# Six open blocks in the first stage of a decoder trunk, with two waits re-ordered around them

## The reference, cut to what matters

```
mod = silu(c) @ ada_w[l] + ada_b[l]            # six vectors: shift, scale, gate, twice
h = rms_norm(x, norm_mix_g[l]) * (1 + scale) + shift
u = h @ w_in                                    # 1024 x 3072: Bg, Cg, xv
z = Cg * xv;  y = (Bg * conv3(z)) @ w_out;  x = x + gate * y
...
q, k, v = projections per head pair; p = softmax(q k^T / 8 + F[t] - F[s]); o = p v
```

## Time and profile before

| | |
|---|---|
| median of 3 runs | 1160.84 us (1160.73 to 1161.4) |
| the profiled execution's own time | 1160.93 us |
| its span, first to last instruction | 1159.1 us |
| PE busy | 1152.2 us (99%) |
| DVE busy | 866.7 us (75%) |
| ACT busy | 543.6 us (47%) |
| mean granted TensorE clock | 1.000 of full speed |

### The profile page before, as it was taken

The page is one execution under the profiler, slowest core; times in us unless marked ns, Lnnn a source line. Parts: engine busy times, 40 slices in busy tenths (PEclk is TensorE's granted clock), DMA queues, the critical chain, the costliest instruction groups (busy, mean ns, idle before and its releaser), DMA issues.

```text
span 1159.1 us, 16337 instructions
## 1 busy us (share of the span) xinstructions
PE 1152.2 (99%) x5840; PEld 967.4 (83%) x5840; DVE 866.7 (75%) x1191; ACT 543.6 (47%) x876; POOL 25.3 (2%) x37
## 2 busy tenths in 40 slices
PE   8999999999999999999999999999999999999999
PEld 6788889988888888888978888888988888888887
DVE  4666988975675675555889889897887778779694
ACT  5322333531331331333677877875675445445521
POOL 2000000000000000200020000000000000000000
DMA  9977655476666666332246555464133323332311
GB/s 296 291 221 230 201 177 185 129 232 187 197 192 191 196 191 189 93 95 87 74 128 141 128 132 129 110 164 145 39 101 116 108 80 105 108 118 83 108 56 73
DMA packets 207324, 168.89 MB, mean 146 GB/s; under 512 B 5684, under 2 KB 180188, under 8 KB 207260
## 3 DMA queue, kind: packets, MB, share of 16 engines
q1 hardware_dynamic: 207068, 167.92, 49.2%
q10 hardware_dynamic: 160, 0.06, 0.0%
q0 software_dynamic: 32, 0.07, 0.0%
HBM read 153.24 MB, written 2.10 MB: 134 GB/s over the span
## 4 chain that ended last, share of the span: by engine, by line
PE 94%; DVE 3%; DMA 1%; ACT 1%; issue 0%; SPq 0%; DVEq 0%
PE bank L787 24%; PE bank L789 23%; PE bank L788 23%; PE bank L1090 4%; PE bank L1089 4%; PE bank L1088 4%; PE bank L1265 2%; PE bank L1247 1%; PE bank L1237 1%; PE bank L1238 1%; PE bank L968 1%; PE bank L969 1%; PE bank L971 1%; DMA ada_first<-in_ada_w 1%; PE bank L926 1%; DMA queries<-qk 0%
## 5 line engine op out<-in xcount | busy, mean ns | idle before, releaser
L787 PE MATMUL bank<-h_hi,w_hi 128*128 128x512 f32 (+1 forms) x848 | 318.8, 376 | 0.3 <-DVE h_lo L1990 0.3
L789 PE MATMUL bank<-h_hi,w_lo 128*128 128x512 f32 (+1 forms) x848 | 316.5, 373 | 0.0
L788 PE MATMUL bank<-h_lo,w_hi 128*128 128x512 f32 (+1 forms) x848 | 316.4, 373 | 0.0
L1403 ACT ACTIVATE w_hi<-raw 128x1024 fp32r<-128x1024 f32 x149 | 156.4, 1054 | 154.6 <-DMA raw<-in_mlp_w 116.7
L1936 DVE TENSOR_TENSOR w_lo<-raw,w_hi 128x1024 fp32r<-128x1024 f32 x149 | 181.4, 1221 | 33.6 <-ACT w_hi L1403 32.7
L787 PEld LDWEIGHTS bank<-h_hi,w_hi 128*128 128x128 f32 x848 | 159.7, 188 | 29.0 <-DVE h_lo L1990 0.8
L789 PEld LDWEIGHTS bank<-h_hi,w_lo 128*128 128x128 f32 x848 | 159.7, 188 | 28.3
L788 PEld LDWEIGHTS bank<-h_lo,w_hi 128*128 128x128 f32 x848 | 159.7, 188 | 27.9 <-issue 0.2
L787 PE MATMUL bank<-g_hi,w_hi 128*128 128x512 f32 (+1 forms) x416 | 154.9, 372 | 0.0
L789 PE MATMUL bank<-g_hi,w_lo 128*128 128x512 f32 (+1 forms) x416 | 153.5, 369 | 0.0
L788 PE MATMUL bank<-g_lo,w_hi 128*128 128x512 f32 (+1 forms) x416 | 153.4, 369 | 0.0
(11 more groups left out here) (291 smaller groups left out, 1683.5 us busy)
## 6 DMA issues: line engine op xcount, KB each, us to landing
raw<-in_mlp_w SPq DMA_DIRECT2D x96, 512.0 KB, 4.0
ada_raw<-in_ada_w SPq DMA_DIRECT2D x40, 1024.0 KB, 5.6
w_raw<-in_mlp_w SPq DMA_DIRECT2D x32, 512.0 KB, 3.3
raw<-in_sc_w_in SPq DMA_DIRECT2D x18, 512.0 KB, 4.2
raw<-in_w_kv SPq DMA_DIRECT2D x16, 512.0 KB, 4.0
ada_first<-in_ada_w SPq DMA_DIRECT2D x24, 256.0 KB, 5.8
raw<-in_q_w SPq DMA_DIRECT2D x8, 512.0 KB, 5.0
keys<-qk SPq DMA_DIRECT2D x16, 256.0 KB, 3.1
```

What stands on the lines that cost most here:

```text
L787: mm(out[:, cols], weights_hi, hi[:, k, cols], start=(k == 0), stop=False)
L788: mm(out[:, cols], weights_hi, lo[:, k, cols], start=False, stop=False)
L789: return mm(out[:, cols], weights_lo, hi[:, k, cols], start=False, stop=(k == KT - 1))
L1403: go(w_hi[:, jj, :, :], raw[:, jj, :, :], ACT.Copy).then_inc(hi_ok, 1)
```

## The change

`FIRST_BLOCKS` goes from 5 to 6: block 5 joins the open blocks, in bank 7, with its weights in `beside_raw`, `beside_hi`, `beside_lo`, loaded, split and used two k tiles at a time like those of block 4. Behind the first stage only blocks 6 and 7 remain before xv; they use slots 1 and 2, and block 7's load is issued in two halves. In the opening the first four x tiles are turned as the rows of x arrive, the products of blocks 3 and 5 come last (`opening_late`) and in full width, ACT copies x tile 7 before 6, and both halves of unit 1's strips stand behind the opening's high products. The row turn goes to bank 4. In the attention loop the value projection runs five k tiles ahead instead of four for i = 1, the third head. The core of the diff:

```diff
-FIRST_BLOCKS = GROUP + 1
-FIRST_BANK = [0, 1, 2, 3, 5]
+FIRST_BLOCKS = GROUP + 2
+FIRST_BANK = [0, 1, 2, 3, 5, 7]
-X_TAKEN = [1, 2, 3, KT, KT - 2]
+X_TAKEN = [1, 2, 3, KT - 1, KT - 2, KT]
+SOON, LATE_BLOCKS = (0, 1, 2, 4), (3, 5)
...
# SP
+                    sp.dma_start(beside_raw[:, 0, k:k + 2, :], first_w[:, k:k + 2, c0 + P:c0 + 2 * P]
+                                 ).then_inc(spare_in[k // 2] if k // 2 < KT // 2 - 1 else beside_in, 16)
...
             sp.wait_ge(first_used, 2)
-            load_block(1, c_g(GROUP + 1))
+            load_block(1, c_g(GROUP + 2))
...
             sp.wait_ge(first_used, 3)
-            load_block(2, c_g(GROUP + 2))
+            sp.dma_start(raw[:, 2, 0:STRIPS, :], c_g(GROUP + 3)[:, 0:STRIPS, :]).then_inc(raw_in[2], 16)
             ada_pair(1, 0, 2, 1)
             sp.wait_ge(hi_ok, KT // 2)
-            sp.dma_start(beside_raw[:, 0, :, :], c_g(GROUP + 3)).then_inc(raw_in[3], 16)
+            sp.dma_start(raw[:, 2, STRIPS:, :], c_g(GROUP + 3)[:, STRIPS:, :]).then_inc(raw_in[3], 16)
...
-                    sp.wait_ge(pe_done, KT + n - 3)
+                    sp.wait_ge(pe_done, KT + n - (2 if n < 3 else 3))
...
# PE
-                for b in range(FIRST_BLOCKS):
+                for b in SOON:
...
+            def opening_late():
+
+                for b in LATE_BLOCKS:
+                    pe.wait_ge(x_ok, X_TAKEN[b])
+                    mm(bank[FIRST_BANK[b]], opening_weights(b), h_hi[:, 0, :], start=True, stop=False, skip_group_check=True)
...
+            for t in range(TT):
+                pe.wait_ge(x_loaded[t], 16)
+                for j in range(4):
+                    one = x_part(j, t)
+                    if t == TT - 1:
+                        one.then_inc(x_turned, 1)
             pe.wait_ge(cols_ok, 2)
-            for j in range(4):
-                x_turn(j)
...
-            unit_strips(1, (0,))
             opening_high(0)
             opening_high(1)
-            unit_strips(1, (1,))
+            opening_late()
+            unit_strips(1)
             opening_low(range(0, 2))
             unit_sum(1)
             opening_low(range(2, FIRST_BLOCKS))
...
-            turn(bank[7][:, 0:ROWS], rows_a[:], ident[0:ROWS, 0:ROWS]).then_inc(cols_pe, 1)
-            for jj in range(FIRST_BLOCKS - GROUP, GROUP - 1):
-                dense(1, jj, h_hi, h_lo)
-            pe.wait_ge(bank_free, GROUP)
-            part_of(KT - 1, 0, bank[GROUP - 1], h_hi, h_lo, range(KT), weights=(beside_hi, beside_lo)).then_inc(pe_done, 1)
+            turn(bank[4][:, 0:ROWS], rows_a[:], ident[0:ROWS, 0:ROWS]).then_inc(cols_pe, 1)
+            for b in range(FIRST_BLOCKS, KT):
+                pe.wait_ge(bank_free, b - 3)
+                part_of(b, b - FIRST_BLOCKS + 1, bank[b - GROUP], h_hi, h_lo, range(KT)).then_inc(pe_done, 1)
...
-                kvq("v", nxt, range(0, 4))
+                ahead = 5 if i == 1 else 4
+                kvq("v", nxt, range(0, ahead))
...
# ACT
+            x_tile(7)
             x_tile(6)
-            x_tile(7)
+            split_first_beside(0)
             for k in range(1, KT):
                 split_first(k)
                 first_tile(k)
+                split_first_beside(k)
             split(1, 1)
-            split(1, 2)
...
# DVE
+                    dve.wait_ge(spare_hi_ok, k // 2 * 2 + 2)
+                    tt(beside_lo[:, 0, k:k + 2, :], beside_raw[:, 0, k:k + 2, :], beside_hi[:, 0, k:k + 2, :],
                        ALU.subtract).then_inc(spare_lo_ok, 1)
...
-            split(1, 1)
-            split(1, 2)
+            split_late(1)
             dve.wait_ge(cols_pe, 3)
-            nc.vector.tensor_copy(cols[:, R_MLP:ROWS], bank[7][:, R_MLP:ROWS]).then_inc(cols_ok, 1)
+            nc.vector.tensor_copy(cols[:, R_MLP:ROWS], bank[4][:, R_MLP:ROWS]).then_inc(cols_ok, 1)
...
             def step_cg(g, jj, j):
                 if j == 1:
-                    split_beside()
-                if j >= FIRST_BLOCKS:
+                    split_late(2)
+                if j > GROUP:
                     split(g, jj + 3)
                 ada_step(g, jj, j, 2)
```

More of the change, by code:

```diff
@@ L302, in yoco_trunk @@
         spare_in = [sem(f"spare_in{q}") for q in range(KT // 2 - 1)]
+        beside_in = sem("beside_in")
         spare_hi_ok = sem("spare_hi_ok")
@@ L940, in unit_sum, with x_part @@
                 one.then_inc(ada_turned, units)
+            def x_part(j, t):
+                return turn(bank[X_BANK[j]][:, t * P:(t + 1) * P], x_rows[:, t, j * P:(j + 1) * P], ident[:])
             def x_turn(j):
@@ L948, in x_turn @@
                 for t in range(TT):
-                    if j == 0:
-                        pe.wait_ge(x_loaded[t], 16)
-                    v = turn(bank[X_BANK[j]][:, t * P:(t + 1) * P], x_rows[:, t, j * P:(j + 1) * P], ident[:])
+                    v = x_part(j, t)
                 v.then_inc(x_turned, 1)
@@ L957, in first_weights @@
                     return first_hi[:, k, b * P:(b + 1) * P], first_lo[:, k, b * P:(b + 1) * P]
-                pe.wait_ge(spare_lo_ok, k // 2 + 1)
-                return spare_hi[:, 0, k, :], spare_lo[:, 0, k, :]
+                if b == GROUP:
+                    pe.wait_ge(spare_lo_ok, k // 2 * 2 + 1)
+                    return spare_hi[:, 0, k, :], spare_lo[:, 0, k, :]
+                pe.wait_ge(spare_lo_ok, k // 2 * 2 + 2)
+                return beside_hi[:, 0, k, :], beside_lo[:, 0, k, :]
             def first_products(k, blocks=range(FIRST_BLOCKS)):
@@ L975, in first_products, with opening_weights @@
                     last.then_inc(first_used, 1)
+            def opening_weights(b):
+                if b < GROUP:
+                    return first_hi[:, 0, b * P:(b + 1) * P]
+                if b > GROUP:
+                    pe.wait_ge(spare_hi_ok, 2)
+                return (spare_hi if b == GROUP else beside_hi)[:, 0, 0, :]
             def opening_high(half):
@@ L981, in opening_high @@
                 pe.wait_ge(*((hh_half, 1) if half == 0 else (hh_ok, H_MIX0 + 1)))
-                for b in range(FIRST_BLOCKS):
+                for b in SOON:
                     if half == 0:
                         pe.wait_ge(x_ok, X_TAKEN[b])
-                    high = first_hi[:, 0, b * P:(b + 1) * P] if b < GROUP else spare_hi[:, 0, 0, :]
-                    mm(bank[FIRST_BANK[b]][:, HALF[half]], high, h_hi[:, 0, HALF[half]], start=(half == 0), stop=False,
-                       skip_group_check=True)
+                    mm(bank[FIRST_BANK[b]][:, HALF[half]], opening_weights(b), h_hi[:, 0, HALF[half]], start=(half == 0),
+                       stop=False, skip_group_check=True)
+            def opening_late():
+                for b in LATE_BLOCKS:
+                    pe.wait_ge(x_ok, X_TAKEN[b])
+                    mm(bank[FIRST_BANK[b]], opening_weights(b), h_hi[:, 0, :], start=True, stop=False, skip_group_check=True)
             def opening_low(blocks):
@@ L1333, in _ @@
                 turn_probs(2 * i)
-                kvq("v", nxt, range(4, 6))
+                kvq("v", nxt, range(ahead, ahead + 2))
                 pe.wait_ge(o_own_ok, 2 * i)
@@ L1337, in _ @@
                 head_sum("q", nxt)
-                kvq("v", nxt, range(6, KT))
+                kvq("v", nxt, range(ahead + 2, KT))
                 pe.wait_ge(normed, NORM_OF["k", nxt] + 1)
@@ L1514, in split_first, with split_first_beside @@
                 go(first_hi[:, k, :], first_raw[:, k, :], ACT.Copy).then_inc(hi_ok if k % 2 else first_hi_ok,
-                                                                             2 if k == KT - 1 else 1)
+                                                                             3 if k == KT - 1 else 1)
                 if k % 2 == 0:
-                    act.wait_ge(*((spare_in[k // 2], 16) if k // 2 < KT // 2 - 1 else (raw_in[0], 32)))
+                    act.wait_ge(*((spare_in[k // 2], 32) if k // 2 < KT // 2 - 1 else (raw_in[0], 32)))
                     go(spare_hi[:, 0, k:k + 2, :], spare_raw[:, 0, k:k + 2, :], ACT.Copy).then_inc(spare_hi_ok, 1)
+            def split_first_beside(k):
+                if k % 2 == 0:
+                    if k // 2 == KT // 2 - 1:
+                        act.wait_ge(beside_in, 16)
+                    go(beside_hi[:, 0, k:k + 2, :], beside_raw[:, 0, k:k + 2, :], ACT.Copy).then_inc(spare_hi_ok, 1)
             def first_tile(j):
@@ L1536, in _, with split_seventh @@
                 first_tile(k)
+                split_first_beside(k)
             split(1, 1)
-            split(1, 2)
-            def split_beside():
+            def split_seventh():
+                act.wait_ge(raw_in[2], 32)
                 act.wait_ge(raw_in[3], 32)
-                go(beside_hi[:, 0, :, :], beside_raw[:, 0, :, :], ACT.Copy).then_inc(hi_ok, 1)
+                go(w_hi[:, 2, :, :], raw[:, 2, :, :], ACT.Copy).then_inc(hi_ok, 1)
             def step_cg(g, jj, j):
@@ L2123, in first_tile @@
                     dve.wait_ge(h_ok, H_MIX0 + j - 3)
```

(17 more changed lines are left out.)

6 lines of the change are left out of this document (4 added, 2 removed).

## The result

The changed kernel takes 1163.65 us (median of 10 runs, 1162.79 to 1164.83) against 1160.88 us for the kernel before (10 runs, 1160.73 to 1161.4): ratio 1.0024, interval 1.0016 to 1.0033. It is slower by 2.8 us. The profiled execution took 1163.72 us, its span is 1161.9 us against 1159.1.

What follows compares the result with a forecast made beforehand. PE was taken to bound the kernel, busy 1152.2 of 1159.1 us. From 1160.93, plus 2.73 for the wait, minus 0.1 for the opening, gave 1163.56, or 1163.5 from the median; range 1160.9 to 1165.3.

Steps and rivals of the forecast that it cites:

- The row turn moves, the work behind it doesn't: Behind the first stage: DVE's list stays tied to the turn, block 8 ready 13.70 us after it, PE waits 2.73 us.
- A wait of 2.7 us: PE before block 8: idle 2.73 us, lost for good; 1.1 to 4.6 us depending on the third ada_raw pair's landing.
- cost nothing extra: Waits ahead of block 8, at blocks 6 or 7: PE would only wait earlier for the same DVE chain.
- The clock, rival (a): After the wait before block 8: PE returns at 1.2 GHz, 2.7 to 5.4 us more, 1166.2 to 1168.9; chance 8%.
- My own case: Whole kernel: one wait of about 2.7 us before block 8, 1162.8 to 1164.1 us around 1163.5; chance 54%.
- Behind block 8: nothing, by a hair: Blocks 10 to 12: block 10's low part just ready in time; 0 lost, bounds 0 and 1 us more.
- rival (b): Blocks 10 to 12: loads land half a microsecond later and PE waits that again, 1164.1 to 1165.5 us; chance 15%.
- The third head: nothing: Third head: one more value step wins nothing, the wait for the queries stays; bounds 0.3 us either way.
- The opening: 0.1 us: Opening: new order wins 0.1 us net, turn of unit 1's sums at 19.72; bounds 0.3 us lost, 0.6 won.
- The tiles: nothing: First stage: block 5's products move in with its copies and DMAs at no net cost; bounds 0.3 us either way.
- The range: Whole kernel's time: 1160.9 to 1165.3 us, said to leave out no more than 2 in 10.
- (c): Block 8 and opening: no wait at block 8 and the opening pays, 1160.2 to 1160.6 us; chance 10%.

Runs made afterwards that it cites:

- The early turn: Changed kernel with the row turn ahead of the last two k tiles of the first stage, in bank 6: 1162.34 us, ratio 1.0012.
- the two experiments with a single wait: Changed kernel with ACT's high part of block 7 after bank 3's copy: 1165.3 us; or block 7's second half-load ahead of the ada_raw pair: 1164.96 us.
- the load-first kernel: Changed kernel with the second half of block 7's load issued ahead of the ada_raw pair: 1164.96 us, ratio 1.0037.
- The five-block version: Kernel before with only the new order of the opening, five blocks staying open: 1160.54 us, ratio 0.9999.
- all mends: Changed kernel with row turn early, block 7's high part behind bank 2's copy and its second half-load ahead of the ada_raw pair: 1160.73 us.

## Why the prediction was right, and where it was not

The forecast was 1163.5, measured 1163.65; direction, size and the place by which it comes are right. By its steps:

- **The row turn moves, the work behind it doesn't.** Right, and this is what decides. Turn at 61.44 (61.5 forecast), third pair at 67.35 (67.4), DVE on at 72.50 (72.8), block 8 ready at 74.92 (75.2). The early turn took away what hangs on it.
- **"A wait of 2.7 us", one wait before block 8.** Its sum was right and its form wrong. Block 8 started 2.46 us later than before, against 2.63 forecast with the opening's gain; but PE waited 1.45 us of it before block 6 and 0.69 before block 8; the rest is the turn's own time (0.2 us) and the end of a product, which work behind it covers when there is no wait. The step that failed is the sentence that waits ahead of block 8 "cost nothing extra". As to the place of block 8 it holds. That the time came out right is luck: the two experiments with a single wait took 1.3 and 1.65 us more.
- **The clock, rival (a).** I gave it 8% and priced it at 2.7 to 5.4 us. Its mechanism is real: a wait of 2.3 or 2.8 us does bring 1.2 GHz. Its size is 1.4 and 1.6 us in the two profiles, seven and eight products, most at 0.43 us, about half of my lower price. In nine of the changed kernel's ten runs the mean granted clock was 1.000, its wait having come in two parts. My own case, a single wait of 2.7 us, no loss at block 12 and the clock kept, is about what the load-first kernel did but for the clock, and it took 1164.96 us, near the top of the range. The Trainium skill, page "TensorE: Matmul & The Clock Gate", section "Why this matters for your kernels", warns of long gaps; the two traces show that gaps shorter than those it warns of, 2.32 and 2.83 us, bring the half clock too.
- **Behind block 8: nothing, by a hair.** Mis-sized: 0 forecast, 0.83 us lost at block 12 (97.56 - 74.97 = 22.59 us for four blocks of 5.44). The load in question landed 7.87 us after its issue, from 87.29 to 95.16, against 6.85 before. With 0.14 us of slack forecast for block 10, such a spread had to count for something: this was rival (b)'s mechanism, at the low end of its price.
- **The third head: nothing.** Wrong by 0.8 us between the two profiled executions, of which 0.6 is the edit with queries in time and 0.2 that they were in time (13.88, 13.68, 13.08 us); wrong by about 0.4 in the medians, which the intervals don't separate from nothing. I read "no idle time" at the turn of the probabilities as "nothing to win there", while a wait just ahead of it, for something else, was covering it.
- **The opening: 0.1 us.** The turn of unit 1's sums is at 19.79 (19.72 forecast) and the idle time before block 5's product is 0.15 us, not 0.4, since PE got there later: it waited 0.41 us for the first `h_hi` instead. The net gain is 0.13 us by the turn (5.39 us later for 5.52 us of products), and only 0.05 if a block counts 5.44 us, as it does in a row of blocks. The sum had a slip of 0.04: 17.29 and a copy of 0.40 give 17.69, where the product started, not 17.65. The five-block version, at 19.02, shows that block 5 eats the gain.
- **The tiles: nothing.** Right: no idle time of PE above 0.06 us from 17.7 us to the row turn, and no loss left with all mends.
- **The range.** It was said to run from the top of (c) to the top of (b), but these are 1160.6 and 1165.5, and 1160.9 and 1165.3 were taken. Nothing hangs on it here.

So in the profiled pair block 12 (+0.83) and the third head (-0.8) cancelled, and a drop of the clock stayed away by the way in which the wait fell. The forecast's number is better than its reasons.

## What to carry to other kernels

When a block of work is moved ahead of a signal, count what still stands between that signal and the next thing that depends on it: here three blocks became two, and a list of 13.5 us on DVE, with a DMA in it that its own steps release, no longer fitted into 11. Here two waits of 1.45 and 0.69 us were cheaper than one of 2.3 or 2.8, because the long one also halved the clock. Mend such waits all together or measure each mend, since taking away the first alone made the kernel slower. And where PE waits for one late thing, ask what the next thing would show if that wait were gone.

## What the runs showed of the hardware

A wait of PE of 2.32 us and one of 2.83 us amid dense products at 2.4 GHz were followed by 1.2 GHz, for 3.4 us, and then by 2.4 GHz again. In the longer one the clock fell 0.36 us before work began again, in the shorter one 0.38 us after. The mean granted clock was below 1.000 in all ten runs of the two kernels with the single wait (0.999, once 0.997), and in one of ten of the changed kernel, whose waits were 1.45 and 0.69 us in its profile: the run of 1164.83 us, its slowest. Why it fell in that run is open, since it has no profile. It was 1.000 in all seven runs without the third head's edit, which have the same waits (1.33, 0.79 and 0.67 us in the profile).

The landing of a like transfer (block 12's weights) varied from 6.7 to 8.1 us between executions. Where PE waits for such a landing, the time hangs on it. That this is why the ten runs of the changed kernel spread over 2.0 us, against 0.7 for the ten of before, is likely and not shown: in another set the kernel before spread over 1.7 us in 27 runs.
